# Two of the three one-hot operands of the first region's odd batches are weighted on GpSimd instead of VectorE

## The reference

```python
q = (hb @ w_q).reshape(C, 8, 2, 128)
s = jnp.einsum('thpd,hpnd->thpn', q, sub_keys)
sv, si = lax.top_k(s, 16)
cand = sv[:, :, 0, :, None] + sv[:, :, 1, None, :]
cidx = si[:, :, 0, :, None] * 128 + si[:, :, 1, None, :]
fv, fpos = lax.top_k(cand.reshape(C, 8, 256), 16)
eidx = jnp.take_along_axis(cidx.reshape(C, 8, 256), fpos, axis=-1)
g = jax.nn.softmax(fv, axis=-1)
a = jax.nn.gelu(jnp.einsum('ted,td->te', u_tab[eidx], hb))
y = jnp.einsum('te,ted->td', g * a, v_tab[eidx])
```

## Time and profile before

| | |
|---|---|
| median of 3 runs | 2017.47 us |
| the profiled execution's own time | 2017.19 us |
| its span | 2015.4 us |
| TensorE busy | 1968.4 us (98%) |
| VectorE busy | 1357.1 us (67%) |
| ScalarE busy | 792.3 us (39%) |
| GpSimd busy | 859.6 us (43%) |
| DMA over the span | 262 GB/s in the mean, about 420 in the second half |

### The profile page before, as it was taken

How to read it: one execution, slowest core, us unless ns; L and a number is a source line. 1 busy time by engine, 2 the same in 40 slices (tenths; PEclk the granted TensorE clock), 3 DMA queues, 4 the chain that set the end, 5 groups by cost and what they waited for, 6 DMA issues and landing times.

```text
span 2015.4 us, 28009 instructions
## 1 busy us (share of the span) xinstructions
PE 1968.4 (98%) x10016; PEld 1448.7 (72%) x10016; DVE 1357.1 (67%) x3001; ACT 792.3 (39%) x1805; POOL 859.6 (43%) x684
## 2 busy tenths in 40 slices
PE   9999999999999999999999999999999999999998
PEld 7888875888868875788886666766666666666564
DVE  3742025333374567749999988888888888887677
ACT  4122233133563326621235555545556555510100
POOL 5444432427543753424425453343344335343333
PEclk9999999999999999999999999999999999999999
DMA  6555652525202411134379999999999999999998
GB/s 233 190 189 180 151 145 94 184 68 178 84 11 58 126 35 53 43 119 134 134 282 356 422 422 422 421 421 422 408 420 421 413 422 416 420 415 417 421 414 298
DMA packets 92920, 527.11 MB, mean 262 GB/s; under 512 B 10080, under 2 KB 14608, under 8 KB 43280
## 3 DMA queue, kind: packets, MB, share of 16 engines
q0 software_dynamic: 37728, 270.55, 33.0%
q1 hardware_dynamic: 49680, 246.95, 33.0%
q10 hardware_dynamic: 5408, 8.34, 2.0%
HBM read 518.46 MB, written 7.34 MB: 261 GB/s over the span
## 4 chain that ended last, share of the span: by engine, by line
DMA 31%; DVE 18%; PE 15%; POOL 4%; issue 2%; ACT 1%; DVEq 0%; POOLq 0%; ACTq 0%
DMA work<-in_peer_uv,consts 16%; DMA ring<-in_peer_uv,consts 15%; PE ps L859 9%; DVE tables L2152 3%; POOL work L2824 2%; POOL ring L2824 2%; DVE ring L2127 2%; DVE work L2127 2%; DVE ring L2109 1%; PE ps L1143 1%; PE ps L888 1%; DVE work L1910 1%; DVE work L1903 1%; DVE tmp L2186 1%; DVE work L1904 1%
## 5 line engine op out<-in xcount | busy, mean ns | idle before, releaser
L1276 PE MATMUL ps<-work,tmp 128*128 128x512 f32 x1008 | 451.4, 601 | 16.4 <-DVE tmp L2186 16.2
L1251 PE MATMUL ps<-hT,work 128*128 128x256 f32 x1984 | 450.2, 381 | 0.0
L1251 PEld LDWEIGHTS ps<-hT,work 128*128 128x128 f32 x1984 | 373.0, 190 | 75.2 <-issue 29.6
L2730 POOL TENSOR_TENSOR w_lo<-ring,w_hi 128x1024 fp32r<-128x1024 f32 (+2 forms) x116 | 275.1, 2378 | 335.3 <-ACT w_hi L2258 335.3
L1276 PEld LDWEIGHTS ps<-work,tmp 128*128 128x128 f32 x1008 | 191.7, 192 | 241.7 <-issue 216.9
L2824 POOL DMA_INDIRECT ring<-in_peer_uv,consts x128 | 203.1, 1587 | 299.0 <-DVE tables L2152 268.5
L2824 POOL DMA_INDIRECT work<-in_peer_uv,consts x128 | 201.5, 1574 | 280.9 <-DVE tables L2152 232.5
L2258 ACT ACTIVATE w_hi<-ring 128x1024 fp32r<-128x1024 f32 (+2 forms) x116 | 120.4, 1041 | 360.4 <-PE ps L859 335.5
L2614 ACT ACTIVATE ring<-iota,consts 128x128 f16<-128x128 f32 x752 | 226.1, 426 | 0.0
L2127 DVE CUSTOM_DVE_ANT_0 ring<-ring,tables 128x1024 f32<-128x1024 f32 x128 | 155.8, 1223 | 72.5 <-DMA ring<-in_peer_uv,consts 71.5
L2127 DVE CUSTOM_DVE_ANT_0 work<-work,tables 128x1024 f32<-128x1024 f32 x128 | 155.7, 1222 | 68.8 <-DMA work<-in_peer_uv,consts 68.1
(11 more groups left out here) (384 smaller groups left out, 3171.6 us busy)
## 6 DMA issues: line engine op xcount, KB each, us to landing
work<-in_peer_v SPq DMA_DIRECT2D x64, 1024.0 KB, 9.1
work<-in_u_steps SPq DMA_DIRECT2D x62, 1024.0 KB, 9.1
ring<-in_a_w_in SPq DMA_DIRECT2D x48, 512.0 KB, 4.0
ring<-in_ada_w SPq DMA_DIRECT2D x48, 512.0 KB, 4.9
ring<-in_peer_w_q SPq DMA_DIRECT2D x32, 512.0 KB, 3.5
ring<-in_a_w_out SPq DMA_DIRECT2D x16, 512.0 KB, 4.1
ring<-in_b_w_in SPq DMA_DIRECT2D x16, 512.0 KB, 4.1
ring<-in_c_in SPq DMA_DIRECT2D x12, 512.0 KB, 3.7
```

The source lines that it names most:

```text
L1251: mm = pe.matmul(ps[:, 4 + s, j * DT:(j + 1) * DT], u[:, s, j, k, :], hT[:, k, GATHERED * P:T], start=(k == 0), stop=(k == KD - 1))
L1276: mm = pe.matmul(ps[:, 2 * t + half, :], tmp[:, s, j * DT + t * P:j * DT + (t + 1) * P], v_ring[:, s, j, half * BANK:(half + 1) * BANK], s ...
L2730: pool.tensor_tensor(w_lo[q % NPIECE][:, 0:n], ring[:, at:at + n], w_hi[q % NPIECE][:, 0:n], ALU.subtract).then_inc(w_split, 1)
```

## The change

- `weighted_j` is no longer called for odd m below 16. GpSimd does its two multiplications for those 8 batches (`weighted_here`), after a wait for `one_hot_j(m)`. The buffers are the same. TensorE waits for VectorE's `one_hot_i(m)` and, in odd batches, for GpSimd (`pool_weighted`).
- On GpSimd, batches 1 and 3 stand ahead of the first gather. The others stand ahead of gathers 1, 2, 4, 5, 6 and 7.
- Late pieces 4 to 7 follow batches 0 to 3 instead of 1 to 4.
- The products between batches are distributed anew (`LATE_AT`): 4 k stand ahead of batch 0 now, after which 5, 8, 7, 7, 2, 3, 1, 3, 2, 3, 1, 3, 2, 3 and 2 follow batches 0 to 14. Before, none stood ahead of batch 0, and 4, 6, 6, 6, 6, 4, then eight times 3, then 0 and 0 followed batches 0 to 15. The last key scores follow batch 3, not 5.

The diff:

```diff
-LATE_AT = (0, 4, 10, 16, 22, 28, 32, 35, 38, 41, 44, 47, 50, 53, 56, 56, 56)
+LATE_AT = (4, 9, 17, 24, 31, 33, 36, 37, 40, 42, 45, 46, 49, 51, 54, 56, 56)
+LAST_SCORES = 3
+WEIGHTED_AHEAD = {1: (5,), 2: (7,), 4: (9,), 5: (11,), 6: (13,), 7: (15,)}
...
@@ tensor
             for b in range(4, NB):
                 pe.wait_ge(bank_free[b], jobs.uses[b])
-            for m in range(RSTEPS):
-                spread_gates(m, m % 2)
-                if LATE_AT[m] == KD * LATE_LEFT + 4:
-                    key_scores("pqL", "peer_l", 2 * PEER_H - 1, 2 * PEER_H - 1)
-                at = LATE_AT[m]
-                while at < LATE_AT[m + 1]:
+            def late_products(at, end):
+
+                while at < end:
                     unit, k = divmod(at, KD)
-                    ks = ALL[k:min(KD, k + LATE_AT[m + 1] - at)]
+                    ks = ALL[k:min(KD, k + end - at)]
                     at += len(ks)
...
+            late_products(0, LATE_AT[0])
+            for m in range(RSTEPS):
+                if m % 2:
+                    pe.wait_ge(pool_weighted, m // 2 + 1)
+                spread_gates(m, m % 2)
+                if m == LAST_SCORES:
+                    key_scores("pqL", "peer_l", 2 * PEER_H - 1, 2 * PEER_H - 1)
+                late_products(LATE_AT[m], LATE_AT[m + 1])
...
@@ vector
             for m in range(RSTEPS):
                 one_hot_j(0, m)
-                one_hot_i(m)
-                weighted_j(m)
-                if 1 <= m <= 4:
-                    late_piece(0, 3 + m)
+                if m % 2:
+                    one_hot_i(m).then_inc(hot_ready, 1)
+                else:
+                    one_hot_i(m)
+                    weighted_j(m)
+                if m < 4:
+                    late_piece(0, 4 + m)
...
@@ gpsimd
             pool.memset(r_y[0], 0.0).then_inc(y_zero, 1)
+
+            def weighted_here(m):
+
+                pool.wait_ge(hot_step, m + 1)
+                for part in range(PARTS):
+                    weight = gT[part][:, m * BATCH:(m + 1) * BATCH].rearrange("p (g t) -> p g t", t=TWIN)\
+                        .unsqueeze(2).to_broadcast([P, BATCH // TWIN, RKEYS, TWIN])
+                    last = pool.tensor_tensor(hot_j[m % 2][part], hot_j[m % 2][1], weight, ALU.mult)
+                last.then_inc(pool_weighted, 1)
+
+            for m in (1, 3):
+                weighted_here(m)
             for h in range(PEER_H):
                 pool.wait_ge(late_placed, h + 1)
                 for i in range(HEAD_STEPS * STEP_ROWS):
                     slot = h * HEAD_STEPS * STEP_ROWS + i
                     k, u = divmod(i, GATHERED)
+                    for m in WEIGHTED_AHEAD.get(slot, ()):
+                        weighted_here(m)
```

More of the change, by code:

```diff
@@ L649, in network @@
         one_made = sem("one_made")
+        pool_weighted = sem("pool_weighted")
         i_kept = sem("i_kept")
@@ L2107, in one_hot_i @@
             def one_hot_i(m):
-                dve.tensor_tensor(hot_i[m % 2], batch_of(iT, m, NKEYS), numbers(0, NKEYS), ALU.is_equal)
+                return dve.tensor_tensor(hot_i[m % 2], batch_of(iT, m, NKEYS), numbers(0, NKEYS), ALU.is_equal)
             def weighted_j(m):
```

## The result

The changed kernel takes 2025.32 us in the median of 7 runs (2023.77 to 2026.75), against 2018.13 us for the kernel before in the same comparison (7 runs, 2015.73 to 2019.64). The ratio is 1.0038, 95% interval 1.0029 to 1.0047: about 7.7 us slower. The prediction was 2030.1 us, range 2019 to 2036. The profiled execution took 2026.75 us with a span of 2025.0 us. It is the longest of the seven, 1.4 us above the median; that of before took 2017.19.

The account below looks back on a forecast made before the run. TensorE, busy for 98% of the span, was taken to bound the kernel. VectorE's -4.7, blocks of +12.7 and +1.3 and a wait of +1.2 made +10.5; with the tail's +2.4, 2017.19 + 12.9 = 2030.1 us, range 2019 to 2036.

Parts of the forecast that it names:

- What to read: Start of the first dense_v, 1058.93 us before: whatever shifts it moves the end by as much.
- Turns at SBUF: VectorE instructions with two SBUF operands and GpSimd's multiplications block each other in turns, so GpSimd's time adds to VectorE's.
- The multiplication, 1.27 us: One GpSimd multiplication, taken from the row of 512 f32 elements; low end 0.8, high end 2.4 us.
- Ten blocks at 1.27, +12.7: Batches 5, 7, 9, 11 and 13 each block VectorE for two GpSimd multiplications: +12.7 us.
- Batches 1 and 3, for which I counted 1.3: Beside pieces 5 and 7, mostly single-input maxima and indices: one of four multiplications counted as blocking, +1.3 us.
- The gathers in front of batch 9, +1.2: Two gathers and the memset delay GpSimd ahead of batch 9; VectorE waits for that batch's buffer, +1.2 us.
- The tail, +2.4: From the end of one_hot_i(15) to the first dense_v: 6.2 us where there were 3.8, +2.4.
- Pieces and products a batch sooner, 0: Same work; four k fill the 1.75 us ahead of batch 0, but waits for odd batches leave nothing: 0.
- The clock, 0 to +4: TensorE's granted clock may fall inside the region at idle gaps: 0 to +4 us, in the range only.
- The one without blocking: Rival: the engines don't block each other, dense_v starts +0.4 to +3 us later, about 2019; chance 0.12.
- The dearer multiplication: Rival: blocking with GpSimd multiplications of 2.0 to 2.4 us, 2042 at 2.0; chance 0.10, shared with a falling clock.
- The faster one: Rival: no blocking and multiplications below 0.8 us, dense_v starts 1 to 3.2 us sooner, 2014 to 2016; chance 0.04.

Follow-up runs that it names:

- e2_gpsimd_alone: Changed kernel with the old order of products and late pieces, GpSimd still multiplying: 2025.42 us, ratio 1.0047 to the kernel before.
- e1_schedule_alone: Changed kernel with all multiplications back on VectorE, new order of pieces and products kept: 2016.28 us against 2016.43 for before, ratio 1.0002.
- e3_writes_only: Changed kernel with two memsets in place of GpSimd's two multiplications per odd batch, queue and semaphores kept: 2016.04 us, ratio 1.0001.
- e6_batches_1_3: Changed kernel with GpSimd multiplying for batches 1 and 3 only, VectorE for the other six odd batches: 2017.76 us, ratio 1.0001.
- e7_gating_between: e1_schedule_alone with the second dot product behind gating(0), not ahead of it: 2018.09 us, ratio 0.9997.

## Why the prediction was right, and where its sizes were off

The forecast was slower by 12.9 us through blocking; measured are 7.7 us through blocking. Step by step:

- **What to read.** That the start of the first `dense_v` moves the end by as much held to within the clock: 7.69 us by the profile, 7.7 by the ratio (7.2 by the medians). That the two figures agree so closely is in part luck: the profiled execution is 9.56 us over that of before (2026.75 - 2017.19), and its parts are 7.69, then 1.23 more in the first `dense_v` (9.76 against 8.53), and 0.52 ahead of the stretch (1013.61 against 1013.09). The last is what single executions differ by: `one_hot_j(0)` starts between 1010.84 and 1013.61 us in the profiles of this study.
- **Turns at SBUF.** Right, and shown by three kernels: `e2_gpsimd_alone` has the loss, `e1_schedule_alone` and `e3_writes_only` don't.
- **The multiplication, 1.27 us.** It takes 1.03 undisturbed. The row of f32 data was the nearest; this form, on 16-bit data, took less; the estimate of 1.11 from the Trainium skill, GPSIMD Engine Reference, section "Elementwise — side-by-side cycle accounting", was the closer one.
- **Ten blocks at 1.27, +12.7: the term that failed.** It charged VectorE with the whole of GpSimd's instruction each time. Three things differ. One block costs mostly 0.81 to 0.84, not 1.03 and not 1.27, as if GpSimd held the reads for that much of its 1.03 only. Only seven of the ten come about by the end of `one_hot_i(15)` (0.81, 0.84, 1.32, 0.84, 0.84, 0.74 and 0.84, together 6.2): twice VectorE stood idle for TensorE while GpSimd multiplied. And this idleness, 1.49 and 1.43 us, is a term that I hadn't (the 1.2 for batch 9 apart). The first of the two comes with GpSimd at batches 1 and 3 alone as well: in `e6_batches_1_3` it is 1.96 us, behind TensorE's wait of 1.32 for batch 1, which stands in the changed kernel too. Batches 1 and 3, for which I counted 1.3, cost 1.2: 0.6 on an integer instruction of the ranking (L1952, 0.81 instead of 0.18) and 0.5 on L2041. With 0.3 on the j of batch 6, it is 6.2 + 1.2 + 0.3 + 2.9 = 10.6 less 4.7, +5.9. Measured are +6.0: what follows `one_hot_i(15)` on VectorE starts 48.04 us into the stretch, where it was 42.04. Predicted were +10.5.
- **The gathers in front of batch 9, +1.2.** The reading had a mistake: by the order of instructions with the change only the two gathers stand ahead of batch 9, and the memset (L2847, at 1047.48) behind it. A wait came, but not there and not for that. GpSimd's pair for batch 9 began at 1045.50, right behind two gathers, 2.0 us after its j was ready; VectorE's wait of 1.43 ended with TensorE's batch 8, which stood behind three k that took 2.91 us instead of 1.54. The wait for the buffer of batch 9 is seen in `e3_writes_only`, 1.42 us.
- **The tail, +2.4.** Measured are +1.7: 5.5 us from the end of `one_hot_i(15)` to `dense_v`, against 3.8. The chain is as I drew it, GpSimd's last pair (3.94 us, the longest, since between its two instructions a dot product of 1.22 got in and not a j of 0.42), TensorE 0.97, ScalarE 0.60, `gating` 0.69.
- **Pieces and products a batch sooner, 0.** Right: 0.3 us in the stretch, not measurable in the time.
- **The clock, 0 to +4.** Right that it would fall inside the region too. At 1042 to 1044 us the granted clock was 0.50, the lower level of 1.2 GHz, behind an idle gap of 1.70, and the three k took 1.37 us more. Behind the gaps of 0.59, 1.98 and 1.20 the three k took their 1.54 us; behind those of 2.00 and 1.51 the first `dense_v` took 1.23 more than before. So the clock, which the sum had at 0, stands in the chain with 1.4 us. These are readings of a profile; no kernel took the clock away by itself, so what the loss would be without it stays open.
- **The rivals.** The one without blocking is out. What it would have cost is shown by `e3_writes_only`, where nothing blocks and GpSimd's queue is almost as full: +0.5 us of stretch, the low end of its +0.4 to +3. The dearer multiplication is out with 1.03 us, and the clock did not fall at each gap. The faster one fell with the blocking: it needed both no blocking and a multiplication under 0.8 us.

The errors did not all run the same way. The blocks came to 6.5 us instead of 12.7, which is 6.2 too much in the forecast; VectorE's idleness, 2.9 instead of 1.2, took back 1.7 of that, and the tail was 0.7 too long. The clock's 1.4 us are inside this, as nearly all of the second idleness. The range held because it reached down to 2019 for the first rival. Its part for blocking began at about 2025, for 0.9 us per block, and that the measured 2025.3 still lies in it is in part luck, since the missing idleness stood against the blocks that didn't come.

Left open: a version that beats both. `e1_schedule_alone`, `e6_batches_1_3` and `e7_gating_between` show that the idleness ahead of batch 0 and ahead of `dense_v` can be filled or shortened by some tenths, and that nothing of it can be measured in the time.

## What to carry to other kernels

Work taken from VectorE and given to GpSimd is not taken away from VectorE while both read SBUF: here 0.34 us of relief by each instruction was paid with 0.8 us of block, and with a slower instruction in TensorE's chain, 1.03 us undisturbed where VectorE takes 0.42. Before such a move, look which neighbours have two operands in SBUF, and try it first with a write-only stand-in of the same length in the same queue, which tells the price of the place from the price of the reading. And when a stage's start is the measure, add the first matmuls behind it, since the granted clock can hide or add more than a microsecond there.

## What the runs showed of the hardware that was not expected

- How long GpSimd kept VectorE out went with what it reads, not with how long it works: 0.83 us for a 1.03 us instruction with two tensors of 512 16-bit elements, 0.41 for a 1.48 us instruction with one, nothing for a 0.95 us memset.
- The hold works the other way too: behind VectorE's i of 1.22 us GpSimd's first multiplication of a pair took 1.96 us instead of 1.04, and the form with one tensor 2.4 instead of 1.48.
- GpSimd's multiplication by a constant with one tensor of 512 f16 elements took 1.48 us undisturbed, the one with two tensors 1.03.
- The two engines don't always take turns: VectorE once lost 1.32 us in the changed kernel, and 2.02 and 2.38 in `e2_gpsimd_alone`, where both of GpSimd's instructions, or the rest of them, went ahead of it.
- An instruction with one tensor operand on VectorE was held up as well: L1952, arithmetic on 32 integers with a constant, took 0.81 instead of 0.18 us beside GpSimd's pair. Maxima and indices beside the same pair kept their 0.50 and 0.29.
